# One decoder trunk kernel: the stick-breaking mixer's q and k transposed by DMA, and its P times V moved from chunk 22 to chunk 30

## The reference

```
z = einsum('bhqd,bhkd->bhqk', qb, k) * scale
log1m = where(mask, log_sigmoid(-z), 0)
between = cumsum(log1m, axis=3, reverse=True) - log1m
a = where(mask, exp(log_sigmoid(z) + between), 0)
o_a = einsum('bhqk,bhkd->bhqd', a, v)
...
p = softmax(q1 k1) - lam * softmax(q2 k2)      # B
o_b = einsum('bhqk,bhkd->bhqd', p, v)
...
merged = sum_i sigmoid(xn @ w_gate[i] + b_gate[i]) * (o_i @ w_branch[i])
x = x + merged @ w_out ; x = x + (silu(hn @ w_ffn_gate) * (hn @ w_ffn_up)) @ w_ffn_down
```

## Time and profile before

| | |
|---|---|
| time, median of 3 | 823.14 us (823.13 to 823.63) |
| the profiled execution: time, span | 822.9 us, 821.1 us |
| PE busy | 814.9 us (99%) |
| DVE busy | 571.7 us (70%) |
| ACT busy | 474.3 us (58%) |
| POOL busy | 291.9 us (36%) |
| products of the chunks (PE acc L726), share of the chain of waits | 80% |
| ACT w_hi waiting for PE | 153.9 us |
| DVE w_lo waiting for ACT's w_hi | 148.0 us |

### The profile page before, as it was taken

One profiled execution on the slowest core, in us unless ns is written; L12 is line 12 of the kernel. 1 busy time (PEld: TensorE's weight loads), 2 busy tenths in 40 slices (PEclk: granted clock), 3 DMA queues, 4 the chain that ended last, 5 costly groups with the idle time before them and its releaser, 6 DMA issues.

```text
span 821.1 us, 10986 instructions
## 1 busy us (share of the span) xinstructions
PE 814.9 (99%) x4012; PEld 669.6 (82%) x4012; DVE 571.7 (70%) x837; ACT 474.3 (58%) x709; POOL 291.9 (36%) x301
## 2 busy tenths in 40 slices
PE   9999999999999999999999999999999999999998
PEld 6888878888888888888888888788788888888886
DVE  5696888868765666655455868898697666666542
ACT  6877655794465555443457785567944645545441
POOL 0079875305203433220000899563070043322100
PEclk9999999999999999999999999999999999999999
DMA  9957768684558778775566757768745698777751
GB/s 329 307 145 226 234 181 223 178 255 142 192 187 237 214 213 210 220 221 181 171 201 230 194 180 219 219 191 208 228 154 187 209 219 213 224 230 208 215 187 70
DMA packets 125766, 169.40 MB, mean 206 GB/s; under 512 B 62865, under 2 KB 65169, under 8 KB 125457
## 3 DMA queue, kind: packets, MB, share of 16 engines
q1 hardware_dynamic: 125424, 168.43, 69.2%
q10 hardware_dynamic: 288, 0.27, 0.1%
HBM read 153.47 MB, written 1.05 MB: 188 GB/s over the span
## 4 chain that ended last, share of the span: by engine, by line
PE 86%; DVE 7%; ACT 4%; issue 2%; DMA 1%; SPq 0%; ACTq 0%; DVEq 0%
PE acc L726 80%; DVE w_lo L1198 3%; ACT eb L1026 2%; PE att L869 1%; ACT w_hi L968 1%; PE att L773 1%; PE att L805 1%; DMA p_halves_t<-p_halves 1%; DVE zg L1232 1%; PE att L890 1%; PE acc L805 1%; DVE eb L1345 1%; DVE cblk L1399 0%; DVE eb L1366 0%; DVE za L1328 0%
## 5 line engine op out<-in xcount | busy, mean ns | idle before, releaser
L1198 DVE TENSOR_TENSOR w_lo<-w_raw,w_hi 128x1024 fp32r<-128x1024 f32 (+1 forms) x276 | 366.6, 1340 | 150.9 <-ACT w_hi L968 148.0
L726 PE MATMUL acc<-w_hi,xt 128*128 128x512 f32 (+1 forms) x1728 | 431.3, 391 | 0.1
L968 ACT ACTIVATE w_hi<-w_raw 128x1024 fp32r<-128x1024 f32 (+1 forms) x275 | 286.2, 1051 | 162.3 <-PE acc L726 153.9
L726 PEld LDWEIGHTS acc<-w_hi,xt 128*128 128x128 f32 x1728 | 319.6, 188 | 65.6 <-ACT w_hi L962 0.8
L726 PE MATMUL acc<-w_lo,xt 128*128 128x512 f32 (+1 forms) x864 | 229.8, 388 | 0.0
L726 PEld LDWEIGHTS acc<-w_lo,xt 128*128 128x128 f32 x864 | 162.0, 188 | 32.7
L1602 POOL COPY hid_t<-hid_halves_t 128x512 uint16<-128x512 uint16 x44 | 34.9, 821 | 96.9 <-DMA hid_halves_t<-hid_halves 82.5
L1593 POOL COPY hid_halves<-hid 128x512 uint16<-128x512 uint16 x44 | 45.6, 1065 | 63.5 <-DVE hid L1277 63.5
L1550 POOL COPY p_halves<-eb 128x768 uint16<-128x768 uint16 x24 | 30.0, 1279 | 97.7 <-DVE eb L1334 60.5
L1463 POOL TENSOR_SCALAR small<-small 128x2 f32<-128x2 f32 (+3 forms) x12 | 8.9, 738 | 149.0 <-ACT sq_dump L1066 134.2
L1610 POOL TENSOR_TENSOR merged<-merged,prod 128x1024 f32<-128x1024 f32 x10 | 32.5, 3255 | 57.9 <-DVE prod L1249 57.1
(11 more groups left out here) (175 smaller groups left out, 717.6 us busy)
## 6 DMA issues: line engine op xcount, KB each, us to landing
w_raw<-in_w_ffn SPq DMA_DIRECT2D x88, 512.0 KB, 4.3
w_raw<-in_w_gate SPq DMA_DIRECT2D x64, 512.0 KB, 4.1
w_raw<-in_w_ffn_down SPq DMA_DIRECT2D x44, 512.0 KB, 4.0
w_raw<-in_w_in SPq DMA_DIRECT2D x39, 512.0 KB, 5.2
w_raw<-in_w_branch SPq DMA_DIRECT2D x16, 512.0 KB, 4.5
w_raw<-in_w_out SPq DMA_DIRECT2D x16, 512.0 KB, 3.3
bg<-in_b_gate SPq DMA_DIRECT2D x8, 512.0 KB, 5.1
w_raw<-in_w_in SPq DMA_DIRECT2D x8, 396.0 KB, 4.3
```

The source lines that it names most:

```text
L726: return pe.matmul(acc[bank0 + t][:, 0:N], x_part[:, k0 + k, t * P:(t + 1) * P], w_part[:, k, 0:N], start=first, stop=last)
L968: act.activation(w_hi[:, n % WR, :, 0:N], w_raw[:, n % RAW, :, 0:N], copy).then_inc(s_hi, 1)
L1198: dve.tensor_tensor(w_lo[:, n % WR, :, 0:N], w_raw[:, n % RAW, :, 0:N], w_hi[:, n % WR, :, 0:N].bitcast(F32), ALU.subtract).then_inc(s_lo, 1)
```

## The change

- q and k of A take the DMA way: `Aq` and `Ak` go; `Adeal` stands at chunk 4, the two DMA transposes at chunk 12 of SP's list, `Ajoin` at chunk 9. The factor of q, formerly part of the ScalarE copy, becomes a GpSimd multiplication in place.
- A's scores and the whole stick-breaking chain stand one chunk later; the dealing of A's P moves from chunk 13 to 18, on GpSimd behind B's preparation; its DMA transposes from 21 and 22 to 27 and 28, its joins on ScalarE from 18 and 19 to 24 and 26.
- `Apv` moves from 22 to 30, ahead of B's scores; A's output split from 23 to 31; `Bpv` of maps 0 and 1 from 28 and 30 to 32.
- The load of `cw`, the compression's weights, moves from 12 to 20.

```diff
-TURN_P = (21, 22, 43, 47, 52, 53, 55, 56)
-TURN_AT = {33: "C", 40: "D"} | {CHUNKS.index(("ffn", j, 3)) + 9: j for j in range(N_FFN)}
+TURN_P = (27, 28, 43, 47, 52, 53, 55, 56)
+TURN_AT = {12: "A", 33: "C", 40: "D"} | {CHUNKS.index(("ffn", j, 3)) + 9: j for j in range(N_FFN)}
...
-    "sig": (49, 53, 57, 57), "o": (23, 45, 48, 58), "subln": 40, "prep": (13, 18, 25), "ngate": 25, "Aq": 6,
-    "Ak": 7, "Asm": (9, 9), "ssig": 10, "sscan": (11, 12), "smul": (12, 13),
-    "Apdeal": (13, 13), "brs": 14, "Apjoin": (18, 19), "Apv": (22, 22), "Bq": 21, "Bk": 21,
-    "Bsm": (22, 22, 30, 30), "Bp": (22, 25, 30, 32), "Bpt": (25, 28, 33, 34), "Bpv": (28, 30, 35, 37), "Bo": 38,
+    "sig": (49, 53, 57, 57), "o": (31, 45, 48, 58), "subln": 40, "prep": (13, 18, 25), "ngate": 25, "Adeal": 4,
+    "Ajoin": 9, "Asm": (10, 10), "ssig": 11, "sscan": (12, 13), "smul": (13, 14),
+    "Apdeal": (18, 18), "brs": 14, "Apjoin": (24, 26), "Apv": (30, 30), "Bq": 21, "Bk": 21,
+    "Bsm": (22, 22, 30, 30), "Bp": (22, 25, 30, 32), "Bpt": (25, 28, 33, 34), "Bpv": (32, 32, 35, 37), "Bo": 38,
...
+    "Bp": 5.5, "smul": 2, "Apdeal": 0.2, "Apv": 3.8,
...
-                    if u == 12:
+                    if u == 20:
                         if l:
...
+                            if a == "A":
+                                pool.wait_ge(proj_out.sem, proj_out.at(l, ("proj", 0)))
+                                settled(pool.tensor_scalar(proj[:, :, SBQ:SBQ + MIX], proj[:, :, SBQ:SBQ + MIX],
+                                                           HD ** -0.5, None, ALU.mult))
+                            if a != "D":
+                                c0 = SBQ if a == "A" else MBQ
+                                srcs = [(proj[:, :, c0:c0 + 2 * MIX], 0, 2 * MIX)]
...
+                            last = {"A": ("sm", ("C", PAIRS["C"] - 1)), "C": ("sm", ("A", PAIRS["A"] - 1)),
+                                    "D": ("sm", ("B", PAIRS["B"] - 1))}[a]
+                            if l or a != "A":
+                                pool.wait_ge(att_done.sem, att_done.at(l - (a == "A"), last))
```

More of the change, by code:

```diff
@@ L128 @@
     "lambda": 2.5, "stats": 1.5, "subln": 6, "Bsm": 4, "Bpt": 6, "ngate": 1.5, "Cp": 3.5, "kcprep": 2, "f": 4,
-    "Bp": 5.5, "smul": 2, "Apdeal": 0.2,
+    "Bp": 5.5, "smul": 2, "Apdeal": 0.2, "Apv": 3.8,
 }
@@ L147, in steps @@
         put(4 * g + 4, "proj", g)
-    for name in ("Aq", "Ak", "Bq", "Bk", "Dc"):
+    for name in ("Bq", "Bk", "Dc"):
         put(PLAN[name], "qk", name)
-    for mixer in "CD":
+    for mixer in "ACD":
         for kind in ("deal", "join"):
@@ L523, in turned @@
         def turned(l, what):
-            if what in ("C", "D"):
-                return 16 * NT * (2 * l + "CD".index(what) + 1)
+            if what in ("A", "C", "D"):
+                return 16 * NT * (3 * l + "ACD".index(what) + 1)
             return 16 * NT * (l * len(range(what % 2, N_FFN, 2)) + what // 2 + 1)
@@ L624, in _ @@
                     if u in TURN_AT:
-                        (turn if TURN_AT[u] in ("C", "D") else turn_hid)(l, TURN_AT[u])
+                        (turn if TURN_AT[u] in ("A", "C", "D") else turn_hid)(l, TURN_AT[u])
                     if chunk(l, u) > 2:
@@ L779, in qk @@
                 bank_free(l, step)
[L780 to L784, removed]
+                if name == "Dc":
                     pe.wait_ge(act_misc.sem, act_misc.at(l, ("ngate", None)))
@@ L787, in qk @@
                     pe.wait_ge(pool_done.sem, pool_done.at(l, ("prep", name[0])))
-                c0 = {"Aq": SBQ, "Ak": SBQ + MIX, "Bq": DFQ, "Bk": DFK, "Cq": MBQ, "Ck": MBK,
-                      "Dq": NSQ}.get(name)
+                c0 = {"Bq": DFQ, "Bk": DFK}.get(name)
                 for m in range(2):
                     for t in range(NT):
-                        if name == "Dk":
-                            src = kdup[:, t, 2 * m:2 * m + 2, :]
-                        elif name == "Dc":
+                        if name == "Dc":
                             src = kcdup[:, t, m, :, :]
@@ L817, in scores @@
                 if n == 0:
-                    if mixer in "CD":
+                    if mixer != "B":
                         pe.wait_ge(joined.sem, joined.at(l, ("join", mixer)))
@@ L1006, in qk_copy @@
                 m = 0 if name[1] == "q" else 2
-                act.activation(qkt[name[0] in "BD"][:, m:m + 2, :].rearrange("p m t -> p (m t)"), att[:, banks_of(step)[0], :], copy,
-                               scale=HD ** -0.5 if name == "Aq" else 1.0).then_inc(read_act.now(step), 1)
+                act.activation(qkt[1][:, m:m + 2, :].rearrange("p m t -> p (m t)"), att[:, banks_of(step)[0], :], copy
+                               ).then_inc(read_act.now(step), 1)
             def pt_free(l, step):
@@ L1526, in _ @@
                         elif kind == "deal":
-                            if a == "C":
-                                srcs = [(proj[:, :, MBQ:MBQ + 2 * MIX], 0, 2 * MIX)]
+                            if a == "A":
[5 more added lines that the diff above has]
+                                srcs = [(proj[:, :, c0:c0 + 2 * MIX], 0, 2 * MIX)]
                             else:
```

2 lines of the change are left out of this document (removed).

## The result

The changed kernel takes 838.93 us (median of four, 838.03 to 838.97), the kernel before 823.13: a ratio of 1.019, 95% interval 1.0172 to 1.0208. The forecast was 833.6 us, range 826 to 841. The sign was right and the time lies in the range, though 0.9 us above the 829 to 838 that the forecast itself was given. Between the two profiled executions (838.03 and 822.9) the loss is 15.1 us where 10.7 were forecast, and 6 of the 15.1 have a cause that the forecast did not name.

What follows compares the result with a forecast made beforehand. TensorE was taken as the bound: chunks times 2.72 us, plus what stands between them, plus waits. First layer +6.65 and second +4.0 on 822.9 gave 833.6 us, range 826 to 841.

Steps and rivals of the forecast that it cites:

- Transposes, -0.95 per layer: Chunks 5 to 8: Aq and Ak, two groups of four TensorE transposes, go, saving 0.95 us per layer.
- The DMA path and A's scores: Before chunk 10: scaling, deal, DMA transposes and join make TensorE wait 1.4 us in the first layer, none in the second.
- the 4.7: GpSimd's deal of A: each copy could sit out a whole VectorE subtraction, 4.7 us instead of 3.5; first layer 1.2 more.
- Chunks 14 to 17: Later stick-breaking chain delays w_lo(16) and w_hi(17): TensorE waits 1.9 us in the first layer, 0.65 in the second.
- Chunk 26: Running balance against the kernel before at chunk 26: +0.85 us in the first layer, -1.8 in the second.
- waits 2.3 before compress: Before compress, chunks 24 to 29: A's joins on ScalarE delay cblk, so TensorE waits 2.3 us (1.4 to 3) per layer.
- The bank before chunk 32: B's products need the bank freed by ot_lo, now after w_lo(33): TensorE waits 2.4 us (1.5 to 3.4) per layer.
- The gap before chunk 34: TensorE's earlier 0.60 us wait for B's last P before chunk 34 is swallowed: -0.6 per layer.
- (1): Rival: bank and cblk are ready when TensorE is, no waits; 821.3 us, or 820.1 without the chunk 34 gaps; chance 0.1.
- (2): Rival: little contention, no wait at chunk 17, 1.6 us at compress, 1.5 at the bank; 826.3 us; chance 0.2.
- (4): Rival: it cancels, with half of (2)'s waits; 822 to 824 us; chance 0.05.
- (3): Rival: transposes hold the loads, costing 3.5 us at first-layer scores, 3 at chunk 17; cblk 3 late; 843 us; chance 0.12.

Runs made afterwards that it cites:

- the tail alone: Kernel before, changed only in A's P: dealt at 18, turned 27 and 28, joined 24 and 26, Apv 30, split 31, Bpv 32; 837.0 us, ratio 1.0162.
- q and k by DMA, first try: Changed kernel with A's P dealt at 14, turned 22 and 23, joined 19 and 20, Apv 22, split 23, Bpv 28 and 30; 838.61 us.
- the half-filled kernel: Changed kernel with five extra products of 512 columns, result unused, ahead of B's products before chunk 32; 835.46 us (834.03 to 836.65).

## Why the prediction was right, and where it was not

- **Transposes, -0.95 per layer**: right, to 0.01 (chunks 5 to 9 are 2.72 apart now).
- **The DMA path and A's scores**: the wait was 0.40 where 1.4 was taken (0 to 3.5). The path is the one forecast, its terms were off both ways. The scaling took 1.50 (0.8 taken, for want of a row), the deal 3.43 (3.5; the 4.7 that the prediction set beside it did not come). The join began 4.63 us after the first transpose was issued, where the earlier trace rows had 5.93, and took 2.26 (2.7 taken). In the second layer no wait, as forecast (join 444.25 to 446.52, TensorE there at 449.0).

```profile
22.75 1.50 POOL L1522 TENSOR_SCALAR proj<-proj 128x512 f32<-128x512 f32 x1 [3.16 <-ACT proj L1031]
24.31 3.43 POOL L1532 COPY halves_in<-proj 128x1024 uint16<-128x1024 uint16 x2
32.40 2.26 POOL L1559 COPY qkt<-halves_t 128x1024 uint16<-128x1024 uint16 x2 [4.66 <-DMA halves_t<-halves_in]
```

  The estimate by the Trainium skill (VectorE: DVE Perf Modes, The three transpose paths) was 21 us for these transposes; the trace does not agree: 4.63 and, in the second layer, 5.00 with issue and landing. (The 14 us of standing that the prediction drew from the 21 leaves out the join; with its 2.7 the estimate would be 16.5.)
- **Chunks 14 to 17**: chunk 16 took 2.05 and 0.8 longer where waits of 1.9 and 0.65 were taken (the waits in it, by their rows, are 1.6 and 0.65). Right, and for the reason given, w_lo(16) and w_hi(17) behind the stick-breaking chain. The slow steps were others than taken: the scans ran at 1.80, as GpSimd began B's preparation only at 50.77, and the multiplication beside it took 2.49 where an earlier one took 0.95 (47.41). That the first layer's chain is late by the load of chunk 12 held too: w_hi(12) stood 3.63 us for it, the masks had to wait for w_lo(12), and the first sigmoid began 1.3 us later against the scores than in the second layer (1.7 forecast).

```profile
34.85 1.06 ACT L961 ACTIVATE w_hi<-w_raw 128x1024 fp32r<-128x1024 f32 x1 [3.63 <-DMA w_raw<-in_w_in]
...
35.94 1.23 DVE L1191 TENSOR_TENSOR w_lo<-w_raw,w_hi 128x1024 fp32r<-128x1024 f32 x1 [3.46 <-ACT w_hi L961]
37.08 0.28 DVE L1314 TENSOR_TENSOR eb<-att,cst 128x128 f32<-128x128 f32 x1
```

- **Chunk 26**: +0.32 and -1.40 where +0.85 and -1.8 stood.
- **Chunks 26 to 30**: +1.8 and +2.0 where +2.7 was forecast, but by another way. The step that failed is "waits 2.3 before compress": TensorE did not wait there, and waited 1.4 ahead of it, 0.6 before chunk 27 and 0.8 before chunk 28. I followed the joins on ScalarE only to w_hi(27), w_hi(29) and cblk, and overlooked that bank TP is freed by ScalarE's copies behind the same joins:

```profile
85.80 0.66 PE L791 MATMUL att<-cst,kcdup 128*128 128x128 f32 x4 [0.61 <-ACT ptb L1084]
...
90.02 0.55 PE L836 MATMUL att<-cst,eb 128*128 128x128 f32 x3 [0.80 <-ACT kcvt L996]
...
86.60 2.00 ACT L1094 ACTIVATE za<-p_halves_t 128x768 uint16<-128x768 uint16 x2
...
89.39 0.58 ACT L996 ACTIVATE kcvt<-att 128x512 f32<-128x512 f32 x1
...
93.79 2.14 DVE L1392 TENSOR_TENSOR cblk<-kcvt,pet 64x240 f32<-64x240 f32 x4
...
96.03 1.10 PE L875 MATMUL att<-cw,cblk 128*32 128x64 f32 x64
```

  TensorE had already lost 1.4 when it came to cblk, and found it 0.1 us old. cblk itself came 1.0 and 1.2 later against the start of chunk 26 where 1.9 was taken (1.2 to 2.4); VectorE's extra wait for w_hi(29) was 0.6 where 0.5 was taken. The run with the joins at 28 and 29 shows both halves of this: the two waits for ScalarE's copies go, and TensorE then waits 0.8 at the forecast place, for cblk.
- **The bank before chunk 32**: 2.71 and 2.73 where 2.4 was taken (1.5 to 3.4), by the named step, ot_lo behind w_lo(33). Right; the runs with B's products at 33 and with the split ahead of w_hi(33) confirm it. "Queued behind the waiting products are chunk 32 and everything after it" was right too, and is what made the next point dear.
- **What a standing TensorE costs afterwards**: missed. The sum priced 2.4 us of waiting at 2.4; it costs 5.7, since B's products and chunk 32 then run at half clock. 3.0 per layer, 6 in all, is more than the 4.4 by which the forecast fell short of the profiled execution. The sum put this term at nothing without saying so. The trace of before could not show it, as its longest wait of TensorE in attention was 0.6; the place for it would have been the range.
- **The gap before chunk 34**: gone, 0.79 where 0.6 was booked.

Together, both layers: 0.1 less than forecast up to chunk 26, 1.6 less between 26 and 30, 6.6 more between 30 and 34, and chunk 4 itself starts 0.35 earlier. That the median lies only 5.3 us above the forecast owes something to luck: what was taken too high between 26 and 30 covers part of what was missing behind it. The rivals: (1) needed ot_lo 2.2 us sooner, and TensorE waited 2.7 for it. (2) and (4) needed small losses at chunk 17 and the bank, and these came a little above the forecast (2.05, 0.8 and 2.7). (3) expected late landings to cost 3.5 at the scores and 3 at chunk 17: chunk 12's load was late, but TensorE came to that chunk only at 41.9, and chunks 10 to 15 run without a wait.

## What to carry to other kernels

When a step moves, list for each bank and buffer who frees it now and what stands ahead of that reader in its own queue; here 8.2 of the 10.9 us of waiting came from such readers (ot_lo, the copies behind the joins), and the products that moved cost what they had cost before wherever the clock was up. A wait of TensorE can have a price beyond its length: one of 2.7 us cost 5.7, while those at which the clock stayed up cost their length. Here the remedies that paid were to place the waiting step a chunk later, to free the bank sooner, and, for the clock's part, to fill the gap with products of no use; splitting one long wait into short ones was not tried. And a gain upstream of a margin that does not move is given back there: lambda's 1.25 us were lost whole at cblk, the joins' 1.8 by half, and cblk's 0.8, in the first layer, at the bank, until the split moved that too.

## What the runs showed of the hardware

- TensorE's granted clock fell from 2.4 to 1.2 GHz after it had stood 2.7 us (both layers of the changed kernel, and of the tail alone) or 3.1 to 3.3 us (q and k by DMA, first try). In the changed kernel it was low for 6.8 us, B's products and most of a chunk ran at half speed, and 3.0 us were lost per layer. After standing 1.6 us it fell too in the half-filled kernel, for 3.4 us, in one layer within the next products and in the other 1.3 us behind their start. The profiled execution with cblk and lambda moved stood 1.6 as well and kept 1.00 (104 to 120 us), while other executions of it took up to 4.1 us longer. The run with lambda alone moved stood 1.5 and 1.1 before compress at a clock of 1.00, and all its five executions had a mean clock of 1.0; the wait of 1.1 for B's preparation lowered nothing either, nor did 1.2 in the profiled execution of the run with cblk at 28. What decides it at 1.6 is open.
- Products whose result nobody uses kept it up: ten of them per layer, in a wait of 2.7 us, saved 5.6 us (838.93 to 833.36).
- The same VectorE steps last longer beside GpSimd: in the changed kernel w_lo(33) took 1.76 beside the joining and dealing copies, w_lo(12) 1.23 with GpSimd at rest (35.94); the multiplication of 128x766 took 2.49 beside B's preparation and 0.95 without.
